# A decoder layer on one core: the sample rows projected in column groups, the second normalisation woven by thirds, and the attention's scores one step ahead

## The reference

```python
mod = silu(c) @ w_ada + b_ada                      # shift, scale, gate, twice
xn = rms_norm(x, norm1_g) * (1 + sc1) + sh1
qa, ka, va, qb, kb, vb, iq, ik, iw = split_proj(xn @ w_in)     # 2888 columns
# RMS norm and rotary on q and k; iq and ik feed an indexer that picks 256 keys a query
# mixer A: 8 heads, three dilated windows merged; mixer B: 8 heads, softmax over the picked keys
x = x + g1 * (concat(oa, ob) @ w_out)
xn = rms_norm(x, norm2_g) * (1 + sc2) + sh2
gate, up = split(xn @ w_gate_up)                   # 2 x 2816 columns
y = x + g2 * ((silu(gate) * up) @ w_down)
```

## Time and profile before

| | |
|---|---|
| median of 3 runs | 1743.2 us (1742.23 to 1745.93) |
| the profiled execution, its own time | 1743.9 us |
| its span, first to last instruction | 1742.3 us |
| PE busy | 1596.6 us, 92% |
| DVE busy | 862.1 us, 49% |
| ACT busy | 682.0 us, 39% |
| POOL busy | 601.2 us, 35% |
| TensorE's mean granted clock | 0.966 of full |

### The profile page before, as it was taken

One profiled execution on the slowest core, in us unless ns is written; L12 is line 12 of the kernel. 1 busy time (PEld: TensorE's weight loads), 2 busy tenths in 40 slices (PEclk: granted clock), 3 DMA queues, 4 the chain that ended last, 5 costly groups with the idle time before them and its releaser, 6 DMA issues.

```text
span 1742.3 us, 29645 instructions
## 1 busy us (share of the span) xinstructions
PE 1596.6 (92%) x10750; PEld 1502.3 (86%) x10750; DVE 862.1 (49%) x1979; ACT 682.0 (39%) x1780; POOL 601.2 (35%) x757
## 2 busy tenths in 40 slices
PE   4697899999978888886998899999999999999998
PEld 3586699999957777774897799999999999999998
DVE  1804889989957878885215332231330322313305
ACT  4424658888267778773223311102111111021111
POOL 2254157666144324205251423313223233132220
PEclk7799899999989999997999999999999999999999
DMA  7700033535252311007412212111111121111002
GB/s 251 276 25 7 2 121 115 183 109 192 77 158 61 98 37 62 8 1 250 162 35 73 73 37 61 38 35 48 48 48 48 36 60 34 38 48 48 0 1 100
DMA packets 138045, 135.30 MB, mean 78 GB/s; under 512 B 7229, under 2 KB 126957, under 8 KB 137302
## 3 DMA queue, kind: packets, MB, share of 16 engines
q1 hardware_dynamic: 111190, 106.43, 19.4%
q10 hardware_dynamic: 25104, 24.64, 4.3%
q0 software_dynamic: 1648, 2.89, 0.6%
HBM read 115.29 MB, written 27.04 MB: 82 GB/s over the span
## 4 chain that ended last, share of the span: by engine, by line
PE 49%; DVE 2%; ACT 1%; DMA 0%; issue 0%; DVEq 0%; ACTq 0%; SPq 0%
PE bank L2447 29%; PE wide L2463 15%; PE bank L2426 5%; DVE xn L2681 0%; DVE alo L2691 0%; DVE rstd L2665 0%; DMA out_y_p<-yn 0%; ACT ahi L2559 0%; PE bank L2487 0%; ACT gwh L2517 0%; PE wide L2408 0%; DVE yn L2735 0%; ACT L2531 0%; ACT L2549 0%; ACT yn L2583 0%
## 5 line engine op out<-in xcount | busy, mean ns | idle before, releaser
L2702 DVE TENSOR_TENSOR hf<-bank,sg 128x352 f32<-128x352 f32 x66 | 34.6, 525 | 464.0 <-PE bank L2447 454.8
L2604 POOL TENSOR_TENSOR hlo<-hf,hhi 128x352 fp32r<-128x352 f32 x66 | 62.6, 948 | 504.3 <-ACT hhi L2533 504.3
L2447 PE MATMUL bank<-ahi,gwh 128*128 128x352 f32 x1056 | 196.4, 328 | 11.5 <-DVE hf L2702 6.6
L2715 DVE SCALAR_TENSOR_TENSOR x<-wide,modT,x 128x352 f32<-128x352 f32 (+1 forms) x264 | 151.3, 573 | 96.8 <-PE wide L2463 96.8
L2447 PE MATMUL bank<-alo,gwh 128*128 128x352 f32 x1056 | 192.2, 324 | 2.5 <-DVE alo L2691 2.5
L2447 PE MATMUL bank<-ahi,gwl 128*128 128x352 f32 x1056 | 193.1, 325 | 0.0
L2447 PEld LDWEIGHTS bank<-ahi,gwh 128*128 128x128 f32 x1056 | 176.4, 190 | 14.2 <-DVE hf L2702 6.9
L2447 PEld LDWEIGHTS bank<-alo,gwh 128*128 128x128 f32 x1056 | 174.3, 189 | 3.0 <-DVE alo L2691 3.0
L2447 PEld LDWEIGHTS bank<-ahi,gwl 128*128 128x128 f32 x1056 | 175.7, 190 | 0.0
L2463 PE MATMUL wide<-hlo,dwh 128*128 128x352 f32 x528 | 171.3, 325 | 0.0
L2463 PE MATMUL wide<-hhi,dwl 128*128 128x352 f32 x528 | 170.4, 323 | 0.0
(11 more groups left out here) (357 smaller groups left out, 3427.4 us busy)
## 6 DMA issues: line engine op xcount, KB each, us to landing
gw<-in_w_gate_up SPq DMA_DIRECT2D x44, 512.0 KB, 5.0
raw<-in_w_ada ACTq DMA_DIRECT2D x14, 1024.0 KB, 9.0
dw<-in_w_down SPq DMA_DIRECT2D x22, 512.0 KB, 3.6
raw<-in_w_ada SPq DMA_DIRECT2D x10, 1024.0 KB, 7.9
raw<-in_w_in ACTq DMA_DIRECT2D x8, 1024.0 KB, 5.6
scr_x<-xT SPq DMA_DIRECT2D x1, 4224.0 KB, 17.1
xnat<-in_x_prompt SPq DMA_DIRECT2D x8, 512.0 KB, 5.9
scr_q<-ubuf SPq DMA_DIRECT2D x32, 128.0 KB, 3.6
```

The lines of the kernel that those rows point to most:

```text
L2447: mm = pe.matmul(pb[2 * s + side][:, 0:THIRD], a[r][:, k, side, :], b[:, k, third(th)], start=(p == 0 and k == 0), stop=(p == 2 and k == K ...
L2604: pool.tensor_tensor(hlo[:, r, third(th)], hf[:, (3 * r + th) % 2, :], hhi[:, r, third(th)].bitcast(F32), ALU.subtract).then_inc(h_lo, 1)
L2702: v.tensor_tensor(hf[:, s, :], pb[2 * s + 1][:, 0:THIRD], sg[:, s, :], ALU.mult).then_inc(h_mul, 1)
L2715: ins = v.scalar_tensor_tensor(out=x1[:, d, cols], in0=src[:, 0:n], scalar=modT[:, 40 + d, 0:1], in1=x1[:, d, cols], op0=ALU.mult, op1=ALU ...
```

## The change

In `front`, the sample rows of chunk `c` (4 to 11) are multiplied as plain float32 in four column groups, ahead of their chunk, from the unsplit weights; ACT copies the result out, and one matmul by `rowsel` sums the groups in place of the 24 matmuls of unit 8. A POOL instruction makes `xsamp`, a DVE instruction `rowsel`. The load that overwrites a weight buffer also waits for `sx_mm`.

```diff
+            def sample_rows(n):
+                c = proj_no[n]
+                pe.wait_ge(raw_in[n % 3], 16 * (n // 3 + 1))
+                pe.wait_ge(pads, 2)
+                for k in range(KD):
+                    j = 32 * (k % 4)
+                    mm = pe.matmul(bank[3][j:j + NSAMP, WCH:2 * WCH], xsamp[:, k, :], raw[:, n % 3, k, :],
+                                   start=(k < 4), stop=(k >= 4))
+                mm.then_inc(sx_mm, 1)
...
+                    if t == NTILE and c >= 4:
+                        pe.wait_ge(sx_relu, 2 + min(c - 2, len(proj) - 4))
+                        pe.matmul(dst[0:NSAMP, :], rowsel[:], samp[:, c % 2, :], start=True, stop=True).then_inc(unit_mm, 1)
...
+                    if t == SAMPLE_AT and 3 <= c < len(proj) - 1:
+                        sample_rows(n + 3)
...
+                        if t == SAMPLE_AT + 1 and c < len(proj) - 1:
+                            act.wait_ge(sx_mm, 2 + c - 2)
+                            act.activation(samp[:, (c + 1) % 2, :], bank[3][:, WCH:2 * WCH],
+                                           ACT.Copy).then_inc(sx_relu, 1)
...
+            v.wait_ge(ik_out, 32)
+            link(v.tensor_reduce(rowsel[:], ident[:].rearrange("p (j r) -> p r j", j=4), AX.X, ALU.add))
```

```diff
-    SETUP_AT = (3, 4, 4, 5, 5, 6)
+    SETUP_AT = (2, 3, 3, 4, 4, 5)
...
-            sp.dma_start(pages[:], A["page_table"].rearrange("n p -> (n p)").unsqueeze(0)).then_inc(pages_in, 16)
+            sp.dma_start(pages[:], A["page_table"].rearrange("n p -> (n p)").unsqueeze(0)).then_inc(small_in, 16)
+            for dst, src in ((expand[:], A["expand"]), (pick[:], A["pick"]), (headsel[:], A["headsel"])):
+                sp.dma_start(dst, src).then_inc(small_in, 16)
...
+            scores(0)
             for n in range(LAST):
-                if n < NSTEP:
-                    scores(n)
+                if n + 1 < NSTEP:
+                    scores(n + 1)
...
-                if n == 3:
+                if n == 2:
                     high_v(0)
...
-            for n in range(NSEQ):
+            for n in range(3):
+                load_window(n)
+            sp.dma_start(mask[:, 0:2, :], A["mask_as"]).then_inc(ldc, 16)
+            for n in range(3, NSEQ):
                 load_window(n)
...
-            pe.wait_ge(ldc, NCONST)
+            pe.wait_ge(small_in, 64)
```

```diff
-                    if u == 3 * KD - 2:
-                        sums(False)
-            sums(True)
+                    if u >= 3 * KD - 2:
+                        sums(u - 3 * KD + 2)
...
+                    if first:
+                        passes = [(0, 0), (0, 1), (1, 0), (1, 1), (0, 2), (1, 2)]
...
+                    if first and th == 0:
+                        sums(2)
...
+            square(KD - 1, 0)
+            square(KD - 1, 1)
+            root(0)
+            normed_high(0, range(0, 4))
+            square(KD - 1, 2)
+            normed_high(0, range(4, KD))
+            root(1)
+            normed_high(1, range(KD))
+            root(2)
+            hidden(0, 0, True, thirds=(0,))
+            split_gate_up(0, 1, True)
...
+            inverse_root(0)
+            normed(0, range(0, 3))
+            residual(KD - 1, 2)
+            normed(0, range(3, KD))
+            normed_low(0)
+            inverse_root(1)
+            normed(1, range(KD))
+            hidden(0, 0, True, (0,))
+            normed_low(1)
+            v.wait_ge(x1_done, 3 * KD)
+            inverse_root(2)
...
+            normed(2, range(KD))
...
+            normed_low(2)
```

More of the change, by code:

```diff
@@ L245, in front @@
     rlS = T.at("rlS", [P, 2, NEWW], F32, T.end)
+    samp = T.at("samp", [P, 2, WCH], F32, T.end - 4 * 2 * NEWW)
+    T.end = UB + 4 * ROWS * WCH + 4 * 2 * NEWW
     LB = T.end
@@ L267, in front @@
     usq = T.at("usq", [P, 4, WCH], BF16, LB + 26624)
+    rowsel = T.at("rowsel", [P, NSAMP], F32, T.end)
     assert T.end <= LB + 28928
@@ L347, in front @@
     SPLIT_AT = 2
+    SAMPLE_AT = 4
     def kind(u):
@@ L1516, in attention @@
     assert T.end <= PERS_END
+    headsel = T.at("headsel2", [P, 8], F32, T.end)
+    pick = T.at("pick2", [P, 2, NSAMP], F32, T.end)
+    assert T.end <= PERS_END
+    expand = T.at("expand2", [NSAMP, 2, P], F32, MIXER_A + 12 * 1024)
+    S.update(headsel2=headsel, pick2=pick, expand2=expand)
     ld = sem("s_load")
@@ L2400, in _, with sums @@
         def _(pe):
-            def sums(last):
-                for th in range(3):
-                    if last:
-                        pe.wait_ge(sq_done, 3 * (KD - 1) + th + 1)
-                    else:
-                        pe.wait_ge(sq_sum, 3 * (KD - 3) + th + 1)
-                    mm = pe.matmul(pb[4 + th][:, 0:THIRD], ones[:], (sq if last else sqsum)[:, th, :],
-                                   start=not last, stop=last)
-                    if last:
-                        mm.then_inc(ssq, 1)
+            def sums(th):
+                pe.wait_ge(sq_sum, 3 * (KD - 3) + th + 1)
+                pe.matmul(pb[4 + th][:, 0:THIRD], ones[:], sqsum[:, th, :], start=True, stop=False)
+                pe.wait_ge(sq_done, 3 * (KD - 1) + th + 1)
+                pe.matmul(pb[4 + th][:, 0:THIRD], ones[:], sq[:, th, :], start=False, stop=True).then_inc(ssq, 1)
             for d in range(KD):
@@ L2523, in split_down, with hidden @@
                 act.activation(dwh[:, r, :], dw[:, r, :], ACT.Copy).then_inc(dw_hi, 1)
-            def hidden(f, r, first, between=lambda th: None):
-                for th in range(3):
+            def hidden(f, r, first, between=lambda th: None, thirds=(0, 1, 2)):
+                for th in thirds:
                     s = (3 * r + th) % 2
@@ L2534, in hidden, with square @@
                     between(th)
+            def square(d, th):
+                act.wait_ge(x1_done, 3 * d + th + 1)
+                if d >= 2:
+                    act.wait_ge(sq_sum, 3 * (d - 2) + th + 1)
+                act.activation((sq if d else sqsum)[:, th, :], x1[:, d, third(th)], ACT.Square).then_inc(sq_done, 1)
             for d in range(KD):
@@ L2540, in _, with normed_high, root @@
                     split_gate_up(0, 0, True)
-                for th in range(3):
-                    m = 3 * d + th
-                    act.wait_ge(x1_done, m + 1)
-                    if d >= 2:
-                        act.wait_ge(sq_sum, 3 * (d - 2) + th + 1)
-                    act.activation((sq if d else sqsum)[:, th, :], x1[:, d, third(th)], ACT.Square).then_inc(sq_done, 1)
-            for th in range(3):
+                if d < KD - 1:
+                    for th in range(3):
+                        square(d, th)
+            def normed_high(th, ks):
+                cols = slice(th * THIRD, min((th + 1) * THIRD, SEQ))
+                for k in ks:
+                    act.wait_ge(xn_a, th * KD + k + 1)
+                    act.activation(ahi[:, k, cols], xn[:, k, cols], ACT.Identity,
+                                   bias=modT[:, 24 + k, 0:1]).then_inc(xn_hi, 1)
+            def root(th):
                 act.wait_ge(ssq, th + 1)
@@ L2695, in hidden @@
-            def hidden(f, r, first):
-                for th in range(3):
+            def hidden(f, r, first, thirds=(0, 1, 2)):
+                for th in thirds:
                     s = (3 * r + th) % 2
@@ new lines, in _, with inverse_root @@
+            for d in range(KD):
+                for g, (k0, _) in enumerate(XG):
+                    if d == k0:
+                        v.wait_ge(x_in[g], 16)
+                for th in range(3 if d < KD - 1 else 2):
+                    residual(d, th)
+            v.wait_ge(o_lo, 3 * KD)
+            v.wait_ge(op_link, 1)
+            def inverse_root(th):
+                v.wait_ge(rs_a, th + 1)
+                v.reciprocal(rstd[:, third(th)], rstd[:, third(th)]).then_inc(rs_d, 1)
+                v.wait_ge(rs_d, th + 1)
```

171 lines of the change are left out of this document (85 added, 86 removed).

## The result

The kernel after took 1751.05 us, the median of 7 runs (1749.03 to 1754.55), beside 1743.2 us for the kernel before. The ratio is 1.0043, with a 95% interval of 1.0032 to 1.0054: it is slower by 0.43%, where 1.5% faster was forecast. The forecast of 1717.2 us and its range up to 1733 us are both wrong.

A forecast was written before the change was run, and what follows sets the result against it. TensorE was taken as the bound (busy 92% of the span), in the attention a chain between engines. 2.3 + 13.3 + 2.9 + 7.5 = 26.0 us; 1743.2 - 26.0 = 1717.2 us, range 1705 to 1733.

The forecast's parts named there:

- Part 2: Attention stage: scores issued a step earlier and the next head's fills a tile earlier, a net gain of 13.3 us.
- the score order: Attention: score issued a step earlier, so DVE's waits for scores at tiles 4 to 6 (2.4 and 1.0 us) go.
- the start: Start of attention: three more DMAs ahead of vn move head 1's queries back, a loss of 1.3 us.
- the earlier fills: Attention: DVE's last key copy moves from tile 6 to 5, taking 0.6 us out of its full stretch.
- Rival (d): Attention: score and all of PE's queue wait for an earlier reduction, 27 us lost, 1758.8 us; chance 0.05.
- Part 1: Front stage, sample rows: float32 products replace a unit of 24 matmuls in eight chunks, a gain of 2.3 us.
- The Trainium skill's factor for 32 columns: Front, sample products: up to four times faster, 8 us more on PE, which DVE's end at 479.78 would swallow.
- Part 3: Sample attention: no wait for headsel, windows start 2.9 us earlier, and all of it reaches the stage's end.
- Part 4: Second normalisation: first reciprocal some 6.0 us earlier, PE ends third 2 8.4 us earlier, of which 7.5 us are counted.

The follow-up runs named there:

- e5: The kernel after with score n back at the start of step n, the earlier fills kept; 1734.3 us, ratio 0.9941 to before.
- e1: The kernel before with the attention part of the change alone (scores a step ahead, earlier fills); 1758.4 us, ratio 1.0103 to before.
- e2: The kernel before with the earlier fills and ACT's earlier first value copy alone, scores in the old order; 1738.7 us, ratio 0.998 to before.
- e11: The kernel after with every score a step ahead but behind the step's transposes, new fills kept; 1745.1 us, ratio 1.0005 to before.
- e8: The kernel after with the loads of expand, pick and headsel moved behind the first vn; 1750.6 us (one run).
- e9: The kernel after with scores ahead only at tiles 4 to 6, behind the transposes, constants behind vn, olo and gwl on DVE; 1722.3 us.
- e7: The kernel after with only the scores of tiles 4 to 6 a step ahead, behind the transposes; 1729.9 us, ratio 0.9919 to before.
- e4: The kernel after with the sixteen olo subtractions of the sample attention on DVE instead of POOL; 1744.6 us, ratio 1.0024 to before.

## Why the prediction was wrong, point by point

**Part 2, the step that failed.** "So DVE leaves tile 6 not 2.4 but about 1.1 us ahead" and, for the other tiles, "This is level". The 1.1 and 0.65 us a head came from a placing of one head's instructions behind each other. At tiles 4 to 6 it was half right: the waits of the earlier trace rows went, and the wait that replaced them was named ("What is late next: DVE's subtraction of the same step") and priced too low. DVE leaves tile 6 later than in the old order, not earlier: of the 0.7 us that a head loses in after against e5, 0.3 arise there. The other 0.4 arise at tile 2, where no reduction had waited for a score in the old order, while the early score, larger and held by a reduction, now stands ahead of the transposes that DVE needs. So where a gain of 1.1 or 0.65 us a head was forecast, the score order costs about 0.7.

The terms: 13.3 us forecast, 12.0 lost in the stage. Of these the score order costs 14.6 (after against e5) to 16.6 (e1 against e2), the start 2.6, and the earlier fills give 5.2 back. Of the fills the prediction said only that they take 0.6 us out of DVE's full stretch. It also counted one of two stretches at half clock as gone, 1.3 us; after has three, and e2 and e5, with the new fills and the old score order, have none behind the start.

**Rival (d)** described the mechanism: the score waits for the reduction of step n - 1 with PE's queue behind it. It priced it at all of tiles 7, 0, 1 and 2, where "This is level" was given a chance of 0.05. The two heads above show it level at tiles 7, 0 and 1, and 0.4 us behind at tile 2 alone: 0.1 us a step over (d)'s 60 steps, where it wanted 0.19 to decide. The rest of the loss, at tiles 4 to 6 and through the lower clock, (d) did not have; the 14.6 us in all are 0.24 us a step. e11 adds what (d) did not say: also behind the transposes the early score costs, then with the values waiting.

**The start.** 1.3 us forecast, bounds 0 to 2.5; measured 2.6 (e5 against e2), of which the constants' place is 0.9 (e8) to 1.4 (e9 against e7). The rest was not told apart. One candidate stands in the traces: TensorE is at the lower clock until 15.7 us behind the stage's start in e5, and until 11.5 in e2.

**Part 1.** The sample product was mis-sized: 2.05 us, but it is 1.0. The prediction took the row of 32 records in the earlier trace rows for one block of `w_ada`. It is two: `order` puts two chunks of `w_ada` behind each late chunk of `w_in` (`order += rest[:2]`), and L592 has 384 records in all, 16 for each of 24 blocks. One block takes half of the 1.95 us, and the sample product, of the same form, takes the same (timeline of PE in after):

```profile
264.06 1.07 PE L619 MATMUL bank<-raw,xsamp 128*32 128x256 f32 x16
265.06 1.22 PE L666 MATMUL wide<-whi,xhi 128*128 128x256 f32 x8
```

PE's busy time from 240 to 480 us fell from 239.1 to 227.9, which is what the prediction's own sum gives with the right term: 2.88 - 1.0 - 0.48 = 1.4 us a chunk, 11.2 over eight. The Trainium skill's factor for 32 columns (TensorEngine Tiling (Array Packing), Theoretical Speedup) was put at 1 us less a chunk, and the trace agrees with that estimate. The further gain on PE was "swallowed", as that sentence said: SP's last stores end at 474.08 (482.44 before), and DVE's last mask ends the stage, at 478.57 for 479.78.

```profile
471.44 2.64 SPq L532 DMA_DIRECT2D out_win_v_s<-ubuf  x8
...
478.27 0.30 DVE L1473 TENSOR_SCALAR mask_sb<-sig 32x288 f32<-32x288 f32 x1
479.50 0.23 SPq L1695 DMA_DIRECT2D pages<-in_page_table  x1
```

The stage's length varies by itself: 480.5, 480.8 and 483.0 in three profiles of the old front, 478.6 to 481.9 in ten of the new. The means, 481.4 and 479.7, make a gain of 1.7 us for 2.3 forecast. No run has part 1 alone, so this compares two sets of kernels that differ elsewhere too.

**Part 3.** The step to the windows came as forecast (5.95 us, gain 3.2 for 2.9). "The rest of the stage follows in order, so 2.9 reaches its end" failed: the scaling of `pr_s` ends with POOL's chain, which starts behind sixteen page loads and did not move. Nothing reached the end (54.4 us, as in e1 and e2 with the old loads). With the chain gone, e4's scaling comes 3.1 us earlier.

**Part 4.** The first reciprocal came 94.5 us behind the stage's start, not 99.8: 5.3 earlier for 6.0. No table load stands between root and squares. DVE's list was right to 0.2 us for each entry but one, the low parts of third 1, 9.0 for 4.0 us. It was set beside DVE's own work only; where POOL's `gwl` would fall was not looked up. PE ended third 2 within 3.3 us of the last low part, as forecast (3.0), but that part came 5 us late, so third 2 ended 3.1 us earlier against the stage's start and not 8.4. The stage gained 3.1 us in this pair of profiles, for 7.5. Its length varies too: the old back took 165.3, 167.3 and 167.1 us (mean 166.6), the new one 160.7 to 163.3 (mean 161.8) where nothing else in it was edited, which makes a gain of 4.7.

**In sum:** 2.3 + 13.3 + 2.9 + 7.5 were forecast. The stages gave, in the two profiles, 3.5 - 12.0 - 2.6 + 3.1 + 0.3 = -7.7 us; the spans differ by 7.8.

## What to carry to other kernels

An instruction that is issued earlier in an in-order queue delays all that it passes. Count its gain only in the steps where its consumer waits for it, and in each step count what stands behind it. Here an early score at three tiles of eight, behind the transposes, gained 5.7 us, and at all tiles, in front of them, it lost 14.6. A wait that is seen in the kernel after is a cost only if the kernel before does not have it at the same place: line up the two heads instruction by instruction. And when a wait is removed or work is moved on VectorE, look at what GpSimd does in that stretch, since one instruction of either may hold the other for all of its length.

## What the runs showed of the hardware that was not expected

- A VectorE scaling of 128x288 floats took 0.37 us alone and 2.37 us (before) to 5.73 us (after) beside a running chain of GpSimd subtractions, the longer the earlier it started. In before and after it ended 0.16 to 0.17 us behind the chain's end, not between two of its sixteen instructions.
- One of eight VectorE instructions with two SBUF inputs took 4.82 us beside a GpSimd subtraction of 4.91 us. In the kernel before the pair met the other way round: the low parts kept their pace, and GpSimd's subtraction took 5.99 us.
- Eight float32 matmuls with 32 stationary columns, in four groups of partitions, took 1.0 us for 256 moving columns, in 16 records; the blocks of `w_ada`, in the same form, take the same (two in 1.95 us).
- The same 32 matmuls with `pick` took 3.74 or 6.09 us by the level of TensorE's clock in that execution: differences of 2 to 3 us between two single profiles can be this and nothing more.
